# Delta rule of a hybrid decoder step: the 64x64 triangular inverse by compact 32x32 diagonal blocks, four array quadrants at a time, and a last level of two small products

## What is computed

```python
lower = jnp.where(strict, jnp.einsum('nbhid,nbhjd->nbhij', kb, kc) * decay, 0.0)
tmat = lax.linalg.triangular_solve(lower + eye, jnp.broadcast_to(eye, lower.shape),
                                   left_side=True, lower=True, unit_diagonal=True)
u = tmat @ (vc * bc[..., None])
w = tmat @ (kb * jnp.exp(gcum)[..., None])
qk = jnp.where(causal, jnp.einsum('nbhid,nbhjd->nbhij', qc, kc) * decay, 0.0)
def step(S, xs):
    v_new = u_i - jnp.einsum('bhck,bhkv->bhcv', w_i, S)
    o_i = (einsum(q_i * exp(g_i), S) + einsum(qk_i, v_new))
    S = S * exp(g_last) + einsum(k_i * exp(g_last - g_i), v_new)
```

## Time and profile before

| | |
|---|---|
| median of 3 runs | 1674.91 us |
| lowest and highest | 1673.93, 1676.64 us |
| span of the profiled execution | 1673.3 us (its own run time is not listed apart) |
| PE busy in the span | 1581.1 us, 94% |
| `delta_rule`, first PE record to the start of the last store | 363.3 to about 550.7 us of the span, 187.4 us |
| mean granted clock of PE | 0.959 |

### The profile page before, as it was taken

How to read it: one execution, slowest core, us unless ns; L and a number is a source line. 1 busy time by engine, 2 the same in 40 slices (tenths; PEclk the granted TensorE clock), 3 DMA queues, 4 the chain that set the end, 5 groups by cost and what they waited for, 6 DMA issues and landing times.

```text
span 1673.3 us, 32210 instructions
## 1 busy us (share of the span) xinstructions
PE 1581.1 (94%) x13700; PEld 1463.9 (87%) x13700; DVE 790.1 (47%) x1409; ACT 412.8 (25%) x710; POOL 239.9 (14%) x279
## 2 busy tenths in 40 slices
PE   7999999989998797898998999999999999999995
PEld 6899998978898655656878999999999999999995
DVE  6359788226766235546663234243342432423426
ACT  5312231322222113545544111101101111111112
POOL 4142000029784001110001000000000000000003
PEclk9999999989999668999998999999999999999998
DMA  6222111212231316024220111201111011111122
GB/s 202 68 41 54 39 40 39 69 45 78 74 84 42 98 19 184 7 77 164 89 102 27 63 38 51 64 26 51 39 51 64 26 51 51 38 63 38 39 102 102
DMA packets 114726, 108.72 MB, mean 65 GB/s; under 512 B 15292, under 2 KB 104839, under 8 KB 114568
## 3 DMA queue, kind: packets, MB, share of 16 engines
q1 hardware_dynamic: 87346, 93.37, 17.7%
q10 hardware_dynamic: 24006, 12.12, 2.7%
q0 software_dynamic: 3232, 1.17, 0.6%
HBM read 94.02 MB, written 12.93 MB: 64 GB/s over the span
## 4 chain that ended last, share of the span: by engine, by line
PE 48%; DVE 3%; ACT 2%; issue 1%; DVEq 0%
PE mf_ps L2618 28%; PE mf_ps L2625 15%; PE mf_ps L2578 3%; PE mf_ps L2606 1%; DVE h_lo L2444 1%; ACT h_hi L2341 1%; PE mf_ps L2646 0%; ACT mo_buf L214 0%; DVE mo_buf L2516 0%; DVE mo_x L2520 0%; ACT mo_buf L2398 0%; DVE ff_scaled L2488 0%; PE mf_ps L2588 0%; DVE ff_w_lo L2451 0%; DVEq L2253 0%
## 5 line engine op out<-in xcount | busy, mean ns | idle before, releaser
L2481 DVE TENSOR_TENSOR ff_acc<-ff_acc,mf_ps 128x344 f32<-128x344 f32 x264 | 135.4, 513 | 185.8 <-PE mf_ps L2625 185.6
L2618 PE MATMUL mf_ps<-h_lo,ff_w_hi 128*128 128x344 f32 x1008 | 213.8, 320 | 0.0
L2618 PE MATMUL mf_ps<-h_hi,ff_w_hi 128*128 128x344 f32 x1008 | 213.6, 320 | 0.0
L2618 PE MATMUL mf_ps<-h_hi,ff_w_lo 128*128 128x344 f32 x1008 | 212.7, 319 | 0.0
L2625 PE MATMUL mf_ps<-ff_h_hi,ff_d_hi 128*128 128x344 f32 x528 | 169.9, 322 | 2.0 <-issue 2.0
L2625 PE MATMUL mf_ps<-ff_h_hi,ff_d_lo 128*128 128x344 f32 x528 | 169.6, 321 | 0.0
L2618 PEld LDWEIGHTS mf_ps<-h_hi,ff_w_lo 128*128 128x128 f32 x1008 | 169.2, 188 | 0.0
L2618 PEld LDWEIGHTS mf_ps<-h_hi,ff_w_hi 128*128 128x128 f32 x1008 | 169.1, 188 | 0.0
L2625 PE MATMUL mf_ps<-ff_h_lo,ff_d_hi 128*128 128x344 f32 x528 | 168.9, 320 | 0.0
L2618 PEld LDWEIGHTS mf_ps<-h_lo,ff_w_hi 128*128 128x128 f32 x1008 | 168.8, 188 | 0.0
L2327 POOL TENSOR_TENSOR ff_x<-ff_x,ff_scaled 128x1024 f32<-128x1024 f32 x7 | 16.4, 2359 | 762.5 <-DVE ff_scaled L2488 762.5
(11 more groups left out here) (442 smaller groups left out, 2528.7 us busy)
## 6 DMA issues: line engine op xcount, KB each, us to landing
fs_keys<-in_cache_k_dram SPq DMA_DIRECT2D x64, 192.0 KB, 2.6
fs_values<-in_cache_v_dram SPq DMA_DIRECT2D x64, 192.0 KB, 2.6
ff_raw<-in_w_gate_dram SPq DMA_DIRECT2D x22, 512.0 KB, 4.0
ff_raw<-in_w_up_dram SPq DMA_DIRECT2D x22, 512.0 KB, 4.1
ff_d_raw<-in_w_down_dram SPq DMA_DIRECT2D x22, 512.0 KB, 5.5
in_raw<-in_w_in_dram ACTq DMA_DIRECT2D x20, 512.0 KB, 3.8
ld_x<-in_x_prompt_dram SPq DMA_DIRECT2D x8, 512.0 KB, 4.3
mo_o_raw<-in_w_out_dram SPq DMA_DIRECT2D x8, 512.0 KB, 5.5
```

The costliest lines, as they stand in the source:

```text
L2481: dve.tensor_tensor(part, part, ps[:, b, 0:TG], ALU.add).then_inc(down_added, 1)
L2618: last = pe.matmul(bank(t % 2 * 3 + g)[:, 0:TG], a[:, k], b[:, k, group(g)], start=(k == 0 and n == 0), stop=(k == KD - 1 and n == 2))
```

## The change

Levels 0 to 4 only touch the two 32x32 diagonal blocks of each 64x64 matrix. After the change they work on tiles of half the width, [128, 6, 32], that hold these blocks alone, one of them in each quarter of 32 partitions, and PE multiplies 32x32 by 32 columns, four quarters one after the other: 24 matmuls a product in place of 12. ACT gathers the blocks out of `lt` (`take_blocks`, four copies, new). Level 5 needs no mask any more: its two products are 12 matmuls of 32x32 each, and its result is copied, not added, into a new full-width tile `tt_full`, into which DVE also writes level 4's diagonal blocks (four small additions in place of half of one large). The minus sign of level 5's mask moves into ACT's copy. POOL clears `tt_full` at the start, loses the sixth mask, and masks the next chunk last and not first in its third step.

```diff
+BLOCK = 32
+LEVELS = 6
+MASKED = LEVELS - 1
...
         tile = [P, 2 * PAIRS, HD]
+        blocks_tile = [P, 2 * PAIRS, BLOCK]
...
-        level = [[put(f"level{s}_{n}", tile) for n in range(2)] for s in range(2)]
-        tt = [put(f"tt{s}", [P, 2, 2 * PAIRS, HD]) for s in range(2)]
-        x = [put(f"x{s}", tile) for s in range(2)]
+        lt_blocks = [put(f"lt_blocks{n}", blocks_tile) for n in range(3)]
+        level = [[put(f"level{s}_{n}", blocks_tile) for n in range(2)] for s in range(2)]
+        tt = [put(f"tt{s}", [P, 2] + blocks_tile[1:]) for s in range(2)]
+        tt_full = [put(f"tt_full{s}", tile) for s in range(2)]
+        x = [put(f"x{s}", blocks_tile) for s in range(2)]
...
+        quarter = lambda e, k: slice(e * HD + k * BLOCK, e * HD + (k + 1) * BLOCK)
+        cols = lambda k: slice(k * BLOCK, (k + 1) * BLOCK)
+        four_up = [(n, quarter(e, k)) for n in range(2 * PAIRS) for e in range(2) for k in range(2)]
...
-                    act.copy(x[s][:], heads(2 * s)).then_inc(x_copied[s], 1)
+                    if lv < LEVELS - 1:
+                        act.copy(x[s][:], x_bank(s)).then_inc(x_copied[s], 1)
+                    else:
+
+                        act.mul(x[s][:], x_bank(s), -1.0).then_inc(x_copied[s], 1)
+
+                def take_blocks(c):
+                    act.wait_ge(lt_done, c + 1)
...
+                    for e in range(2):
+                        for k in range(2):
+                            act.copy(lt_blocks[c % 3][quarter(e, k)], lt[c % 3][quarter(e, k), :, cols(k)]).then_inc(
+                                blocks_done, 1)
...
+                    if r == 2 and new is not None:
+                        take_blocks(new)
...
+                for s in range(2):
+                    pool.memset(tt_full[s][:], 0.0).then_inc(zeroed, 1)
...
-                        if hi is not None:
-                            mask(hi, 5)
...
-                        if new is not None:
-                            mask(new, 0)
                         if lo is not None:
                             mask(lo, 3)
                         if after is not None:
                             keep(after)
+                        if new is not None:
+                            mask(new, 0)
...
+                    if lv < MASKED - 1:
+                        last = dve.tensor_tensor(tt[s][:], tt[s][:], t_bank(s), ALU.add)
+                    elif lv == MASKED - 1:
+
+                        if c >= 2:
+                            dve.wait_ge(uw_done, c - 1)
+                        dve.tensor_tensor(tt[s][:, 0], tt[s][:, 0], t_bank(s)[:, 0], ALU.add)
+                        for e in range(2):
+                            for k in range(2):
+                                q = quarter(e, k)
+                                last = dve.tensor_tensor(tt_full[s][q, :, cols(k)], tt[s][q, 1], t_bank(s)[q, 1], ALU.add)
+                    else:
+                        for e in range(2):
+                            last = dve.tensor_copy(tt_full[s][quarter(e, 0), :, cols(1)], t_bank(s)[quarter(e, 0), 1])
+                    last.then_inc(t_added[s], 1)
...
+                        for n, e in pair_up:
+                            last = pe.matmul(x_bank(s)[quarter(e, 1), n], lt[c % 3][quarter(e, 0), n, cols(1)],
+                                             tt[s][quarter(e, 0), 0, n], start=True, stop=True)
...
+                    if lv < MASKED:
+                        for n, q in four_up:
+                            pe.matmul(t_bank(s)[q, 0, n], tt[s][q, 1, n], x[s][q, n], start=True, stop=True)
+                        for n, q in four_up:
+                            last = pe.matmul(t_bank(s)[q, 1, n], x[s][q, n], tt[s][q, 1, n], start=True, stop=True)
```

More of the change, by code:

```diff
@@ L120, in constants @@
     m.block_later = put("block_later", [P, P])
-    m.levels = put("levels", [P, 6, HD])
+    m.levels = put("levels", [P, MASKED, BLOCK])
+    m.eye32 = put("eye32", [P, BLOCK])
     m.cum64 = put("cum64", [P, HD])
@@ L360, in _ @@
                     pool.dma_start(t[:], m.tables[s]).then_inc(const_in, 16)
-                for l in range(6):
-                    pool.dma_start(m.levels[:, l], m.tables[8 + l, :, 0:HD]).then_inc(const_in, 16)
+                for l in range(MASKED):
+                    pool.dma_start(m.levels[:, l], m.tables[8 + l, :, 0:BLOCK]).then_inc(const_in, 16)
                 for n, t in enumerate((m.cum64, m.eye64, m.keep64)):
                     pool.dma_start(t[:], m.tables[8 + n, :, HD:P]).then_inc(const_in, 16)
+                pool.dma_start(m.eye32[:], m.tables[11, :, HD:HD + BLOCK]).then_inc(const_in, 16)
                 pool.wait_ge(cleared, 2)
@@ L1313, in _ @@
                             if lo >= 2:
[L1314 to L1316 removed]
+                                pool.wait_ge(t_added[s], of_level(lo - 2, LEVELS - 1))
+                            pool.wait_ge(level_ready[s], of_mask(lo, 0))
+                            pool.tensor_tensor(tt[s][:, 1], level[s][0][:], over_blocks(m.eye32[:]), ALU.add).then_inc(
                                 tt_init[s], 1)
@@ L1354, in _ @@
                 dve.wait_ge(state_zero, 1)
+                dve.wait_ge(zeroed, 2)
                 def add_level(c, lv):
@@ L1461, in lower_times_t @@
                     s = c % 2
-                    pe.wait_ge(level_ready[s], of_level(c, lv))
                     if of_level(c, lv) > 1:
                         pe.wait_ge(t_added[s], of_level(c, lv) - 1)
-                    for n, e in pair_up:
-                        rhs = tt[s][half(e), 0, n] if lv > 0 else m.eye64[half(e)]
-                        last = pe.matmul(heads(2 * s)[half(e), n], level[s][lv % 2][half(e), n], rhs, start=True,
-                                         stop=True)
+                    if lv < MASKED:
+                        pe.wait_ge(level_ready[s], of_mask(c, lv))
+                        for n, q in four_up:
+                            rhs = tt[s][q, 0, n] if lv > 0 else m.eye32[q]
+                            last = pe.matmul(x_bank(s)[q, n], level[s][lv % 2][q, n], rhs, start=True, stop=True)
+                    else:
+                        for n, e in pair_up:
+                            last = pe.matmul(x_bank(s)[quarter(e, 1), n], lt[c % 3][quarter(e, 0), n, cols(1)],
+                                             tt[s][quarter(e, 0), 0, n], start=True, stop=True)
                     last.then_inc(x_done[s], 1)
@@ L1476, in next_t @@
                         pe.wait_ge(q_copied, c + 1)
-                    if lv < LEVELS - 1:
-                        for n, e in pair_up:
-                            pe.matmul(heads(2 * s)[half(e), n], tt[s][half(e), 1, n], x[s][half(e), n], start=True,
-                                      stop=True)
-                    for n, e in pair_up:
-                        last = pe.matmul(heads(2 * s + 1)[half(e), n], x[s][half(e), n], tt[s][half(e), 1, n],
-                                         start=True, stop=True)
+                    if lv < MASKED:
+                        for n, q in four_up:
+                            pe.matmul(t_bank(s)[q, 0, n], tt[s][q, 1, n], x[s][q, n], start=True, stop=True)
+                        for n, q in four_up:
+                            last = pe.matmul(t_bank(s)[q, 1, n], x[s][q, n], tt[s][q, 1, n], start=True, stop=True)
+                    else:
+                        for n, e in pair_up:
+                            last = pe.matmul(t_bank(s)[quarter(e, 0), 1, n], x[s][quarter(e, 1), n],
+                                             tt_full[s][quarter(e, 1), n, cols(1)], start=True, stop=True)
                     last.then_inc(tt_done[s], 1)
@@ L1533, in values_and_keys @@
                     for n, e in pair_up:
-                        pe.matmul(heads(stage[0])[half(e), n], tt[s][half(e), 1, n], vb[half(e), n], start=True, stop=True)
+                        pe.matmul(heads(stage[0])[half(e), n], tt_full[s][half(e), n], vb[half(e), n], start=True, stop=True)
                     for n, e in pair_up:
-                        last = pe.matmul(heads(stage[1])[half(e), n], ke[half(e), n], tt[s][half(e), 1, n], start=True,
+                        last = pe.matmul(heads(stage[1])[half(e), n], ke[half(e), n], tt_full[s][half(e), n], start=True,
                                          stop=True)
@@ L2709, in tables @@
     t[7] = np.where(col <= row, 0, NEG)
+    j, n = row % BLOCK, i[None, :BLOCK]
+    for l in range(MASKED):
+        s = 1 << l
+        t[8 + l, :, :BLOCK] = -((j // (2 * s) == n // (2 * s)) & (n // s % 2 == 1) & (j // s % 2 == 0)).astype(np.float32)
+    t[11, :, HD:HD + BLOCK] = j == n
     j, n = row % HD, i[None, :HD]
-    for l in range(6):
-        s = 1 << l
-        t[8 + l, :, :HD] = -((j // (2 * s) == n // (2 * s)) & (n // s % 2 == 1) & (j // s % 2 == 0)).astype(np.float32)
     t[8, :, HD:] = j <= n
```

37 lines of the change are left out of this document (22 added, 15 removed).

## The result

The changed kernel takes 1727.13 us (median of 4, 1722.37 to 1731.41), the kernel before 1674.42 us on the same chip (median of 4, 1672.34 to 1676.64). The ratio is 1.031, 95% interval 1.029 to 1.033: 3.1% slower, where I had forecast 1650 us and a range that ends at 1683. The profiled execution has a span of 1720.6 us, 47.3 longer than before.

The account below looks back on a forecast made before the run. PE was taken to bound the steady part of `delta_rule` at 20.03 us a double chunk; window terms +0.8, -3.5, -5.0, -12.9, -2.5, -1.5 and 0 give -24.6, so 1674.9 becomes 1650.3 us, range 1640 to 1683.

Parts of the forecast that it names:

- Price of a product: On PE, a product of levels 0 to 4 goes from 0.70 to 0.38 us, bounds 0.35 to 1.40.
- Changing the shape: On PE, each change of tile shape costs 0.14 us; nine more per double chunk, +1.3 us.
- The other engines: Per steady double chunk POOL 13.8, DVE 13.0, ACT 5.7 us busy, all under PE's new time, costing no throughput.
- The stall of the earlier trace: Window from 407 to 432 us: 1.8 of the 4.7 us stall given back, within that window's -5.0 us.
- PE per steady double chunk, 16.5 us: PE's steady time: 20.0 less 4.8 for cheaper products plus 1.3 for shape changes; 16.8 with 0.3 added for DVE.
- Rival (c): PE's records can't be issued faster than 29.2 ns: double chunk 30.4 us, 1755 us in all; chance 0.08.
- Rival (d): Granted clock falls inside the phase with less to stream: about 1678 us, or 1740 if throughout; chance 0.04.
- (a): DVE's tail or dearer shape changes (0.20) hold the double chunk at about 17.8 us: 1658 us; chance 0.15.
- (b): Only two 32x32 tiles run at once on PE: product 0.75 us, double chunk 21.3, 1681 us; chance 0.13.

Follow-up runs that it names:

- e9: Kernel before, with every product of levels 0 to 4 issued once more ahead of itself with a single column: 1747.80 us, ratio 1.044.
- e5: Kernel before plus a phase of its own where TensorE alone multiplies 32x32 blocks on four tiles, 8 then 32 columns: 1731.78 us.
- e3: Changed kernel with matmuls of levels 0 to 4 streaming 64 columns for five of six heads, same record count: 1721.54 us, ratio 1.029.
- e1: Changed kernel issuing only the first 32x32 block of each head in levels 0 to 4 from the third chunk on: 1672.51 us, ratio 1.001.
- e2: Changed kernel with masks, T, its transpose and X of levels 0 to 4 in bfloat16, one record per matmul: 1656.97 us, ratio 0.990.
- e8: Kernel before with VectorE transposes replacing products at levels 0 to 4, level 5 as two 32x32 products, no sixth mask: 1654.22 us, ratio 0.988.
- e6: Changed kernel without the loads of keys from the second sample on: 1716.37 us, ratio 1.024.
- e7: Changed kernel with T made from its transpose by VectorE in place of one product per level, levels 0 to 4: 1668.87 us, ratio 0.997.

## Why the prediction was wrong

Point by point, by its own steps.

- **Price of a product**: right in size, 0.41 us against 0.38, bounds 0.35 to 1.40. Its working was wrong, so the size came out partly by luck: I took 53.8 of the 58.3 ns of a record for columns and 4.5 for what stays. e9 shows a 64x64 tile where one column costs 28 ns a record, nearly as much as 64, and e5 shows 32x32 tiles where 8 and 32 columns are alike (13.3 ns at the lower clock). So fewer columns alone would have gained next to nothing. A smaller tile alone would not either: in e3, with 64 columns on 32x32 tiles, a record takes 13.4 ns, 54 in its own tile, where 64x64 had 58. Only both together give the 34 ns (8.5 x 4) of the changed kernel. Why a small tile with few columns is cheaper was not measured by itself. The earlier trace rows had the price of one column already: L1720's records of one column on 64x64 tiles cost 53 ns at the half clock, where twice the 29.2 of 64 columns would be 58.4.
- **Changing the shape**: right in size. The trace after has 149 ns between the last 64x64 record and the first 32x32 one, where the starts within a 64x64 group are 7 and 52 ns apart by turns, so a change costs some 0.1 us beyond the usual step; 0.14 was taken, and e1, with all of the changes, has a double chunk of 17.96 us.
- **The other engines**: right, as shown above. The stall of the earlier trace rows went away, too: DVE's `kept` is 476 ns on average, and its one long instance, 1.97 us at 528.07, has no engine listed as waiting for it.
- **PE per steady double chunk, 16.5 us**: this is the step that failed. It sums array time and assumes that records come as fast as the array takes them, 7.9 ns each. They do within 128 (8.5); over a longer run they come at 27.6 ns (e5). By that figure 895 records need 24.7 us of supply, and took 27.5: stretches whose 128 records have more work than 3.5 us of their own (the 64x128 and 128x384 ones) don't give back what the dense ones lose, and the clock adds up to 0.9 (e3). Before, 128 records took 20.03/583 x 128 = 4.4 us on average, so the supply was hidden. There was less to spare than the average says: the shortest of the 19 packets in its four steady windows took 3.68 us.
- **Rival (c), chance 0.08**, is what happened in kind: "issue" as the bound. Its size was off, 30.4 us and 1755, where 27.5 and 1727 were measured, for it took today's 29.2 ns, an array time, as the floor of issue. The argument that set it aside, four records of L1994 that start within some 20 ns, was true and looked at too short a run; the prediction even noted "they may have waited in the queue". The Trainium skill, "TensorEngine Tiling (Array Packing)", Instruction Overhead, pointed to the same side by another mechanism, a minimum of about 60 cycles a matmul. e9's one column at 28 ns a record agrees with a price that narrow columns do not lower; over four tiles the 1.2 us a product that the prediction estimated from it is not what the trace has (0.41).
- **Rival (d)**: the clock did fall, to between 0.81 and 0.87 in the steady windows and 0.67 in the drain. The three longest stretches at 1.2 GHz in the steady windows begin at 449.2, 503.8 and 531.1, 0.7 to 1.4 us behind the end of a break in which TensorE had idled more than 1.5 us, and e3, whose breaks are shorter (20.4 us in all against 24.9), has 1.00 in three of its four windows. I take the fall for a result of the breaks, worth about 0.9 us of 7.4 per double chunk by e3; that it can't carry the loss is shown, which of the two comes first is not. In the drain (25.6 us against 17.3) its share was not measured.
- **Rivals (a) and (b)**: PE's waits in the steady windows name no VectorE instruction, and two tiles at once are out by the 0.41 us.

The sum closes: 27.45 less 20.03 is 7.4 us in each of four windows, 3.0 in the window before them (where the stall of the earlier trace rows was given back), 3.1 in the first 47, 8.3 and 2.0 in the drain: 46 of the 47.3 us of span.

Not settled: what fills the 1.2 to 1.5 us behind a fetch, and what sets the time from the entry of a packet to the next fetch, which is 1.1 us in e5 and 1.5 on average before the breaks of e2.

## What to carry to other kernels

Count TensorE's records as well as its array time: for each run of 128 (256 instructions, 16 KB) take the larger of its array time and 3.5 us (3.6 to 4.1 in the kernels above), run by run and not on average. Making tiles smaller multiplies records; once a float32 64x64 kernel stands at 34 ns a record, as here, the gain is in fewer records (a product that another engine can give, as VectorE's transpose did in e8), not in shorter ones. Look at the page's row of instruction packets and for "issue" in the waits before and after.

## What the hardware showed that I had not expected

- TensorE's instructions come at 16 KB per 3.53 us when nothing else runs (e5), with the array idle half of the time; taking away nearly all data transfers beside it changed the double chunk by 0.4 us (e6). A packet is fetched only behind the entry of the one before, also where nothing waits (the kernel before).
- Four 32x32 tiles take float32 records every 8.5 ns together, and a record on 64x64 tiles costs 28 ns with 1 column and 28 to 30 with 64 (e9).
- VectorE's transpose of 32x32 blocks costs little more than an addition of the same size: 578 ns against 530 for 128x384 in e8, 375 against 352 for 128x192 in e7.
